# Unscaled rows at the head of the second block and of its feed-forward, and 32 KB rows for the expert weights

## The reference, cut to what matters

```python
# first block, its end: h is (272, 1024), then only the last 256 rows
h = h + expert_choice_ffn(rms_norm(h, ffn_norm_g), w_router, w_gate, w_up, w_down)
#   for each of 16 experts, on its 34 chosen rows xg:
#   y = (silu(xg @ w_gate) * (xg @ w_up)) @ w_down ;  scattered back with the gate's weights
x = rms_norm(h, final_norm_g)[16:]

# second block
h1 = rms_norm(x, norm1_g)
proj = h1 @ w_in          # first 1536 columns: dn_qkv, then a causal convolution of 4 taps and silu
...                       # four branches, gates, merged
x = x + merged @ w_out
h2 = rms_norm(x, norm2_g)
x = x + square(relu(h2 @ w_ff1)) @ w_ff2
```

## Time and profile before

| | |
|---|---|
| median of 3 runs | 1717.28 us (1716.75 to 1719.55) |
| the profiled execution's own time | 1717.86 us |
| its span in the profile | 1716.1 us |
| TensorE busy | 1481.4 us (86%) |
| VectorE busy | 564.4 us (33%) |
| ScalarE busy | 413.9 us (24%) |
| GpSimd busy | 107.6 us (6%) |
| moved from memory | 509.23 MB |

### The profile page before, as it was taken

One profiled execution on the slowest core, in us unless ns is written; L12 is line 12 of the kernel. 1 busy time (PEld: TensorE's weight loads), 2 busy tenths in 40 slices (PEclk: granted clock), 3 DMA queues, 4 the chain that ended last, 5 costly groups with the idle time before them and its releaser, 6 DMA issues.

```text
span 1716.1 us, 18717 instructions
## 1 busy us (share of the span) xinstructions
PE 1481.4 (86%) x7789; PEld 880.6 (51%) x7789; DVE 564.4 (33%) x966; ACT 413.9 (24%) x850; POOL 107.6 (6%) x117
## 2 busy tenths in 40 slices
...
GB/s 383 114 105 239 293 427 427 427 427 427 427 427 427 426 427 427 427 427 427 427 426 427 427 427 427 291 135 131 134 111 36 126 116 152 181 123 185 184 201 142
DMA packets 55989, 511.50 MB, mean 298 GB/s; under 512 B 6481, under 2 KB 6737, under 8 KB 28897
## 3 DMA queue, kind: packets, MB, share of 16 engines
...
HBM read 509.23 MB, written 1.05 MB: 297 GB/s over the span
## 4 chain that ended last, share of the span: by engine, by line
PE 56%; DMA 35%; DVE 4%; ACT 3%; issue 1%; POOL 0%; ACTq 0%; DVEq 0%; SPq 0%; POOLq 0%
DMA sb_ring<-in_w_gate_up 33%; PE PS L771 10%; PE PS L690 7%; PE PS L728 7%; PE PS L1118 6%; PE PS L807 4%; PE PS L788 4%; DMA sb_raw<-in_w 2%; PE PS L880 2%; PE PS L600 2%; PE PS L707 2%; PE PS L787 2%; PE PS L490 1%; PE PS L493 1%; PE PS L498 1%
## 5 line engine op out<-in xcount | busy, mean ns | idle before, releaser
L690 PE MATMUL PS<-sb_ring,sb_XG 128*64 128x512 f32 x2048 | 466.4, 601 | 120.3 <-DMA sb_ring<-in_w_gate_up 120.0
L690 PEld LDWEIGHTS PS<-sb_ring,sb_XG 128*64 128x64 f32 x2048 | 142.7, 137 | 438.4 <-issue 228.8
L2010 DVE TENSOR_TENSOR sb_SL<-sb_SL,PS 128x512 f32<-128x512 f32 x32 | 20.5, 683 | 792.4 <-PE PS L690 792.4
L728 PE MATMUL PS<-sb_ring,sb_HT 128*64 128x512 f32 x1024 | 226.1, 595 | 28.6 <-DMA sb_ring<-in_w_down 14.1
L1991 DVE TENSOR_TENSOR sb_wp<-sb_raw,sb_wp 128x1024 fp32r<-128x1024 f32 x160 | 206.7, 1294 | 115.2 <-ACT sb_wp L1307 113.9
L1307 ACT CAST sb_wp<-sb_raw 128x1024 fp32r<-128x1024 f32 x160 | 166.9, 1045 | 124.4 <-PE PS L1118 56.3
L771 PE MATMUL PS<-sb_hr,sb_wp 128*128 128x256 f32 x1440 | 183.7, 289 | 6.2 <-DVE sb_hr L2041 3.5
L771 PEld LDWEIGHTS PS<-sb_hr,sb_wp 128*128 128x128 f32 x1440 | 178.5, 196 | 10.0 <-issue 6.5
L728 PEld LDWEIGHTS PS<-sb_ring,sb_HT 128*64 128x64 f32 x1024 | 82.0, 137 | 162.4 <-issue 116.3
L1319 ACT ACTIVATE sb_SL<-PS 128x512 f32<-128x512 f32 x32 | 17.4, 595 | 516.8 <-PE PS L690 516.8
L788 PE MATMUL PS<-sb_hr,sb_wp 128*128 128x512 f32 x256 | 90.0, 405 | 3.4 <-DVE sb_hr L2041 3.4
...
## 6 DMA issues: line engine op xcount, KB each, us to landing
...
sb_raw<-in_w SPq DMA_DIRECT2D x160, 512.0 KB, 4.0
...
```

Of the source, the lines that this page charges most:

```text
L690: ins = e.matmul(PS[64 * g:64 * g + 64, b, :], m.XG[:, k, r0:r0 + 64], m.ring[s][:, (2 * g + q) * 512:(2 * g + q) * 512 + 512], start=(k = ...
L728: ins = e.matmul(PS[64 * g:64 * g + 64, b, :], m.HT[:, c % 8, (c // 8) * 64:(c // 8) * 64 + 64], m.ring[s][:, a * 1024 + g * 512:a * 1024 ...
```

## The change

It has three parts.

1. **Rows of 32 KB.** `fetch_four` takes the place of `fetch_pair`: four slots with one transfer of 4 MB, a row of 32 KB for each partition, with the weights laid out so on the host. The groups of the first fill, two groups after it and the last one of the stream (`PAIRS`) stay in pairs, and the last pair is still fetched in halves.
2. **The second block begins on rows that its norm has not scaled.** The rows h are turned as they are, multiplied by both gains together (`g1`), split into `hTu`, and six tiles (`EARLY`) are computed from these. Meanwhile the scales are worked out; a product of ones with a diagonal matrix (`ZD`) puts each row's scale into every partition (`ZB`). The six tiles are multiplied by `ZB` in `cb` before their taps; for tiles 6 to 11 and `nat`, `hT` is made from the turned rows times gain times `ZB`. The last expert's `Y` is copied in two halves by two engines, ahead of the weight pieces; GpSimd makes `lo(0)` to `lo(2)`; VectorE looks six pieces ahead.
3. **The feed-forward runs on unscaled rows throughout.** `square(relu(s*v)) = s*s*square(relu(v))` for a positive s, so the sums of squares are taken beside the `ff1` tiles, and one over the mean is applied in the last addition. The parts of `hT` are made straight from the turned rows in PSUM, and a tile waits for each k apart.

The core of the diff:

```diff
+PAIRS = tuple(range(16, 24 + RING, 4)) + (16 + 24 * 16 - 4,)
+EARLY = 6
 def brought(i):
+    if i - i % 4 not in PAIRS:
+        return i - i % 4
     return i if i - i % 2 in HALVED else i - i % 2
...
+    def fetch_four(i, src):
+        for j in range(4):
+            if brought(i + j) == i + j:
+                n = sum(brought(i + q) == i + j for q in range(4))
+                s, o = ring_slot(i + j), 2048 * j
+                for q in range(n):
+                    for event in freed(i + j + q):
+                        sp.wait_ge(*at(*event))
+                e.dma_start(m.ring_four[s // 4][:, o:o + 2048 * n], src[:, o:o + 2048 * n])...
...
+    def tile_early(i, bank):
+        v = [x.rearrange("p (k c) -> p k c", k=8) for x in piece(P_QKV + i)]
+        b = room(bank, "qkv", i)
+        for k in range(8):
+            pe.wait_ge(*at("early hi", k))
+            pe.wait_ge(*at("early lo", k))
+            for q, (p1, p2) in enumerate(PASSES):
+                ins = e.matmul(PS[:, b, 0:256], v[p1][:, k, :], m.hTu[p2][:, k, :], ...)
...
+    for i in range(EARLY):
+        tile_early(i, 4 + i % 4).then_inc(*mark("pe_c_proj", "in", "qkv", i))
+        if i == 2:
+            b = room(7, "scales")
+            pe.wait_ge(*at("diagonal", 0))
+            pe.wait_ge(*at("diagonal", 1))
+            e.matmul(PS[:, b, 0:256], m.ones, m.ZD, start=True, stop=True)...
+    for i in range(EARLY, 12):
         tile_hT(P_QKV + i, "qkv", i).then_inc(*mark("pe_c_proj", "in", "qkv", i))
...
     # ScalarE, last expert: Y first, then hi(0) to hi(2)
+        if ex < NE - 1:
+            e.copy(m.Y[64 * par:64 * par + 64, 512:1024], PS[64:128, 4, :])...
+    for n in range(3):
+        hi(n)
+    for k in range(8):
+        act.wait_ge(*at("in", "h1", k // 2))
+        e.mul(m.hTu[0][:, k, :], PS[...], m.g1[:, k:k + 1]).then_inc(*mark("act_norm2", "early hi", k))
+    hi(3)
...
     # VectorE, convolution
     for i in range(12):
-        lo(i + 3)
+        lo(i + 6)
...
         dve.wait_ge(*at("out", "qkv", i))
+        if i < EARLY:
+            e.tensor_tensor(cb[:, 3:259], cb[:, 3:259], m.ZB, ALU.mult)...
...
     # GpSimd
+    for n in range(3):
+        pool.wait_ge(*at("hi", n))
+        e.tensor_tensor(m.wp_lo[n], m.raw[n], m.wp_hi[n].bitcast(F32), ALU.subtract)...
...
     # VectorE, last addition
-            e.tensor_tensor(hv, hv, PS[:, banks.of("ff2", ti, db), :], ALU.add)...
+            dve.wait_ge(*at("h2 scale", ti))
+            e.scalar_tensor_tensor(hv, PS[...], m.fr[:, 8 + ti:9 + ti], hv, ALU.mult, ALU.add)...
```

319 lines of the change are left out of this document (162 added, 157 removed).

## The result

The changed kernel takes 1695.64 us (median of four runs, 1694.43 to 1699.81), the kernel before 1718.41 us beside it. The ratio is 0.9873, 95% interval 0.9853 to 0.9892: faster by 1.3%. The forecast was 1695.5.

What follows compares the result with a forecast made beforehand. The weight stream was taken to bound the experts, TensorE with gaps ahead of it the stages behind. Experts -1.3, second block's start -10.1 and feed-forward -10.4 made -21.8 off 1717.28: 1695.5 us, range 1687 to 1706.

Steps and rivals of the forecast that it cites:

- experts: Experts' stage with 32 KB rows: faster stream, later start and longer tail together, -1.3 us.
- The rate: Experts' weight stream: 32 KB rows halve the number of rows, each with a fixed cost; -7.7 us, bounds 6.2 to 9.2.
- Rival 1: Experts' weight stream: a 32 KB row moves no faster than two of 16 KB; 1703 us, chance 0.10.
- rival 2: Experts' weight stream: a row costs less than assumed, so the stream gains 2.6 us; 1700.5 us, chance 0.08.
- The pause: Start of the experts' whole-group stream: DMA engines run dry near 214 us; +3.5 us, bounds 0 and 4.8.
- The end: End of the experts: TensorE gets the last `gate_up` group whole, so `down` starts and ends later; +2.9 us.
- The start of the second block: From the last `down` rows to the step behind `lo(23)`: tiles on unscaled rows start sooner; -10.1 us.
- VectorE takes back 8: Second block's start: TensorE alone would give -18 us, but VectorE's slower pace per tile loses 8 of that.
- Rival 4: Second block's start: VectorE sets the pace less than thought; up to 5 us more gain, 1690 us, chance 0.09.
- rival 3: Second block's start: GpSimd blocks VectorE or the clock stays low; gain 4 to 5 us, about 1701.5, chance 0.12.
- Rival 5: Experts: the ring of five groups is too coarse and the stream breaks; slower, some 1725 us, chance 0.05.
- The feed-forward: From output product to first feed-forward result: tiles start without waiting for the norm; -10.4 us, -8 if the clock drops.

Runs made afterwards that it cites:

- pairs_all: Changed kernel with every group of the experts' weights sent as two transfers of 16 KB rows: 1697.6 us, ratio 0.9883 to the kernel before.
- rows8: Changed kernel with all experts' weights sent slot by slot in 8 KB rows: 1710.4 us, ratio 0.9954 to the kernel before.
- pairs_start: Changed kernel with its first three whole groups (slots 44 to 55) sent as pairs: 1697.4 us, ratio 0.9859 to the kernel before.
- taps_out: Changed kernel with three of four convolution taps left out in the second block's twelve tiles, values no longer the reference's: 1689.6 us.
- early4: Changed kernel with four tiles on unscaled rows instead of six: 1698.7 us, ratio 0.9886 to the kernel before.
- tap0_act: Changed kernel with the first convolution tap of tiles 6 to 11 moved from VectorE to ScalarE: 1695.0 us, ratio 0.9871 to the kernel before.
- warm_half: Changed kernel with four filler products on TensorE ahead of most waits for whole groups, last expert included except its last groups: 1697.8 us.
- ff_before: Changed kernel with only the feed-forward's norm put back as before the change: 1709.4 us, ratio 0.9954 to the kernel before.
- warm: Changed kernel with eight filler products on TensorE ahead of most waits for whole groups in experts 1 to 14: 1731.8 us.
- best: Changed kernel with pairs in slots 44 to 55 and the last three groups, half fillers, first tap on ScalarE, nat copies before rounding: 1692.1 us.

## Why the prediction was right

**The time** was right to 0.1 us, partly by luck. Two terms came out 1.7 us better each than forecast (experts, start), and the middle, which had no term, took 2.2 back. The gain was 22.8 us instead of 21.8, from a median before of 1718.4 instead of 1717.28.

**The rate** (-7.7) was mis-sized a little. Down to the landing of the last `gate_up` weights the stream gained 6.35 us with 2.3 lost in the pause, so 8.7, inside the stated bounds of 6.2 to 9.2. (With the roundings that the prediction names, 418.5 to 419.5 against 426 to 427, the bounds come to 6.6 and 8.7, so the measured gain is at their edge.) Rival 1 fell by the 431 GB/s and by `pairs_all`; rival 2 by the 420 GB/s of `rows8`. The Trainium skill (DMA: Bandwidth & Descriptors, section "Why small descriptors are slow (HBM only)") would have 0.3% for this halving; the runs show 1%, from 427 to 431, and the measurement decides.

**The pause** (+3.5) was right in kind and place. It measured 2.3: before the change the last weights of that group were issued at 216.95 and landed at 227.35, after it they were issued at 216.13 and landed at 229.6. `pairs_start` removed it.

**The end** (+2.9) measured +3.3: from the last `gate_up` landing to the end of `down` it was 21.7 us and is now 25.0. The path was named only in part. I let TensorE's 7.3 us of the last group set the start of `down`. That alone would put it at about 1079.4, and it waited for the landing of the `down` group until 1080.23. The cause is the same, coarse groups. What I had not seen is that idle pieces twice as long also cost clock. The stage ends anywhere from 1094.2 to 1096.9 in the profiled executions with whole groups to the end. In the four latest of them (`taps_out`, `early4`, `tap0_act`, `warm_half`) the last `gate_up` group took 8.5 to 8.8 us instead of 7.09; that moved the end by 0.9 us or less, since in the changed kernel `down` had to wait 0.8 us for its landing anyway. The rest of the spread is a later landing of the last `gate_up` weights, 1069.2 to 1071.5, whose cause is open.

**The start of the second block** (-10.1) measured -11.85. The first steps were right within a microsecond: first tile at 6.5 after zero, the early ones without a gap, a wait of about 1 us beside the scales. What was off is VectorE's pace, forecast at 3.56 and 3.11 us a tile: it was 3.42 and 2.96, and the convolution ended at 62.3 instead of 66. And "VectorE takes back 8", whose absence the prediction named as a sign of being wrong, is too strong. `taps_out` says 5.3, and `tap0_act` that the last 2 of VectorE's microseconds are free, since TensorE is as late. The forecast's own sum had a slip here: 9.9 + 11 x 2.87 + 8 x 2.73 + 2.9 is 66.2, so by TensorE alone it would be -19.5, not -18, and VectorE's share 9.4. That the new order of this stretch gives its 11.85 us is read from the two traces; no run undoes part 2 alone. Rival 4 has some truth, rival 3 none: with GpSimd subtracting for 7.09 us beside them (3 x 2.4), VectorE's early parts took 0.40 us each. That agrees with the Trainium skill (SBUF — State Buffer, section "SBUF: two separate sides"), by which VectorE and GpSimd exclude each other only where VectorE's operation has two SBUF inputs or runs in a two-port mode. Rival 5 did not come up either: the middle of the experts never lost its rate.

**The feed-forward** (-10.4) measured -10.7, with tile 0 in place at 6.4 after zero and the granted clock at 1.00; `ff_before` gives 10.9 from the other side.

**Open** is the middle of the second block. It is 338.0, 338.4 and 338.5 us in the three kernels without whole groups, and 339.2 to 344.3 in the eleven with them. The mean granted clock of 1170 to 1510 us is 0.98 in `pairs_all` and `rows8`, 0.97 in the changed kernel, 0.96 in `pairs_start`; each piece at 0.50 costs at most half its length. By `warm`, in its one profiled execution, it isn't the clock among the experts. By the traces' records of the clock TensorE spends 13.7 us of the middle at 1.2 GHz in the three kernels, 17.1 in the changed one and 23.9 in `pairs_start`; at half speed that explains up to 1.7 of the 2.2 us and 5.1 of the 6. But `ff_before`, `taps_out`, `tap0_act` and `best` have 13.7 too, and 339.2 to 340.8 us. With one profiled execution each it could be chance; no run tells it apart.
